# Narrow reciprocals and split float32r scores in the first attention of an encoder step

## The reference

```python
q = rope(q.reshape(b, t, N_HEADS_A, HEAD_DIM), pos)
k = rope(k.reshape(b, t, N_KV_A, HEAD_DIM), pos)
...
logit = jnp.einsum('bqgrd,bqkgd->bqgrk', qg, k_sel).astype(jnp.float32) * (HEAD_DIM ** -0.5)
logit = jnp.where(valid[:, :, None, None, :], logit, -jnp.inf)
p = jax.nn.softmax(logit, axis=-1).astype(v_sel.dtype)
o = jnp.einsum('bqgrk,bqkgd->bqgrd', p, v_sel)
```

## Time and profile before

| | |
|---|---|
| median of 3 runs | 1536.83 us (1536.07 to 1537.23) |
| the profiled execution's own time | 1536.02 us |
| its span in the trace | 1534.2 us |
| busy: PE / PE weight loads / DVE / ACT / GpSimd | 1491.9 / 1372.8 / 1081.5 / 635.9 / 580.2 us |
| chain that ended last, by engine | PE 86%, DVE 7%, ACT 2%, issue 2%, DMA 1% |
| granted TensorE clock, mean | 0.992 |
| first attention, from the first scores to the last products with values | 183.2 to about 290 us |

### The profile page before, as it was taken

How to read it: one execution, slowest core, us unless ns; L and a number is a source line. 1 busy time by engine, 2 the same in 40 slices (tenths; PEclk the granted TensorE clock), 3 DMA queues, 4 the chain that set the end, 5 groups by cost and what they waited for, 6 DMA issues and landing times.

```text
span 1534.2 us, 29121 instructions
## 1 busy us (share of the span) xinstructions
PE 1491.9 (97%) x11413; PEld 1372.8 (89%) x11413; DVE 1081.5 (70%) x2033; ACT 635.9 (41%) x1265; POOL 580.2 (38%) x346
## 2 busy tenths in 40 slices
PE   5999999999999999999999999999999999999998
PEld 2768955899999999999888888887999999999998
DVE  1559899768887878877634444457997877688753
ACT  3434366434552145532533333334254541355423
POOL 1234842134762066632222222231228640376421
PEclk8999999999999999999999999999999999999999
DMA  9874510232354433443254444442542355333521
GB/s 334 266 266 150 140 38 1 83 97 69 84 148 143 149 92 88 122 151 88 63 180 128 127 126 126 126 127 76 171 114 56 86 163 179 84 110 83 153 82 62
DMA packets 244455, 189.23 MB, mean 123 GB/s; under 512 B 12888, under 2 KB 228608, under 8 KB 240112
## 3 DMA queue, kind: packets, MB, share of 16 engines
q1 hardware_dynamic: 231232, 178.61, 38.8%
q10 hardware_dynamic: 13104, 8.97, 1.9%
HBM read 175.44 MB, written 8.50 MB: 120 GB/s over the span
## 4 chain that ended last, share of the span: by engine, by line
PE 86%; DVE 7%; ACT 2%; issue 2%; DMA 1%; POOL 0%; SPq 0%; POOLq 0%; ACTq 0%; DVEq 0%
PE lin L859 40%; PE lin L1438 28%; PE lin L876 6%; PE S L1200 2%; PE O L994 1%; PE O L1253 1%; DVE acc_out L2655 1%; PE O L1329 1%; PE T L1233 1%; DMA ada_raw<-in_w_ada 1%; PE S L1119 1%; PE S L1063 1%; DVE rinv_w L2555 1%; PE lin L1297 1%; PE S L1275 1%
## 5 line engine op out<-in xcount | busy, mean ns | idle before, releaser
L2145 POOL TENSOR_TENSOR w_lo<-w_raw,w_hi 128x1024 fp32r<-128x1024 f32 (+3 forms) x68 | 168.3, 2477 | 407.5 <-ACT w_hi L1610 407.5
L2236 POOL TENSOR_TENSOR w_lo<-ada_raw,w_hi 128x512 fp32r<-128x512 f32 x114 | 156.8, 1377 | 241.6 <-ACT w_hi L1911 241.6
L1610 ACT ACTIVATE w_hi<-w_raw 128x1024 fp32r<-128x1024 f32 (+2 forms) x110 | 125.1, 1139 | 225.0 <-PE lin L859 212.3
L859 PE MATMUL lin<-act_hi,w_hi 128*128 128x288 f32 (+1 forms) x1088 | 164.5, 302 | 6.1 <-ACT act_hi L1642 2.0
L859 PE MATMUL lin<-act_hi,w_lo 128*128 128x288 f32 (+1 forms) x1088 | 167.3, 299 | 0.2
L859 PEld LDWEIGHTS lin<-act_hi,w_hi 128*128 128x128 f32 (+1 forms) x1088 | 149.2, 189 | 16.6 <-issue 10.1
L859 PE MATMUL lin<-act_lo,w_hi 128*128 128x288 f32 (+1 forms) x1088 | 162.1, 298 | 0.0
L859 PEld LDWEIGHTS lin<-act_hi,w_lo 128*128 128x128 f32 (+1 forms) x1088 | 150.0, 188 | 7.5 <-issue 6.7
L859 PEld LDWEIGHTS lin<-act_lo,w_hi 128*128 128x128 f32 (+1 forms) x1088 | 149.6, 188 | 3.4 <-issue 2.9
L2236 POOL TENSOR_TENSOR w_lo<-s_tmp,w_hi 128x512 fp32r<-128x512 f32 x76 | 129.1, 1717 | 15.0 <-ACT w_hi L1914 14.9
L1438 PE MATMUL lin<-act_hi,w_hi 128*128 128x288 f32 x608 | 105.4, 295 | 0.0
(11 more groups left out here) (348 smaller groups left out, 3042.0 us busy)
## 6 DMA issues: line engine op xcount, KB each, us to landing
ada_raw<-in_w_ffn_in SPq DMA_DIRECT2D x76, 512.0 KB, 5.2
w_raw<-in_w_ffn_out SPq DMA_DIRECT2D x32, 704.0 KB, 4.8
ada_raw<-in_w_ada SPq DMA_DIRECT2D x20, 1024.0 KB, 7.8
ada_raw<-in_w_ada SPq DMA_DIRECT2D x32, 512.0 KB, 4.9
w_raw<-in_w_in_b SPq DMA_DIRECT2D x32, 512.0 KB, 4.2
w_raw<-in_w_in_a SPq DMA_DIRECT2D x16, 512.0 KB, 6.1
ada_qo<-in_w_ada SPq DMA_DIRECT2D x8, 1024.0 KB, 7.3
ada_raw<-in_w_ada_final SPq DMA_DIRECT2D x16, 512.0 KB, 5.6
```

Of the source, the lines that this page charges most:

```text
L859: last = nc.tensor.matmul(lin_u(u)[0:m, tok], w, (lo if p == 2 else hi)[:, at(t) if at else t, tok], start=(p == 0 and t == 0), stop=(p == ...
L1610: A(w_hi[:, u % 2, 0:n], w_raw[:, u % 2, 0:n], ACT.Copy).then_inc(whi_done, 1)
L2145: TT(w_lo[:, u % 2, 0:n], w_raw[:, u % 2, 0:n], w_hi[:, u % 2, 0:n].bitcast(F32), ALU.subtract)\
L2236: TT(ring(w_lo, q), raw, ring(w_hi, q).bitcast(F32), ALU.subtract).then_inc(ws_lo_p, 1)
```

## The change

1. Reciprocals. DVE makes them narrow (two or three columns, `recip_a`) and, after the softmax reads of unit n+2, copies them 64 times side by side (`widen_a`).
2. Scores. `kT4` becomes float32r and holds for each key head its high part on one half of the partitions and its low part on the other. A query head is needed on both halves: `q_hi` and `q_lo0`/`q_lo1` hold, for each of a pair's heads, the high and the low part on all 128 partitions. A score is then two float32r matmuls over 128 rows (high queries, low queries). The sample tokens of both heads lie side by side and make one product and one softmax read of 128 rows. `q_hi` and `q_lo0` share memory with `ada_raw`.
3. Who makes the parts. Keys: ACT the high parts (`k_high`, as many copies as before), GpSimd the low parts (`k_low`). Queries: pairs 0 to 2 by ACT (`q_high`) and DVE (`q_lows`: for pair 0 in the top-k rounds, for pairs 1 and 2 at the end of loop steps 0 and 2); pairs 3 to 7 by GpSimd (`q_split`, ahead of `split_pair` of the pair three before). The part on the other 64 partitions is brought by four DMAs a pair on the SP queue (`q_double`): pair 0's ahead of the load of U_Q+7, pair 1's ahead of the swap of U_Q+7, the others behind it.
4. The first `sum_load` waits for all scores (`s_done`) instead of `ada_used`.

```diff
+        q_hi = sb("q_hi", [P, 2, 2 * TOK], F32R, scope=s)
+        q_lo0 = sb("q_lo0", [P, 2 * TOK], F32R, scope=s)
...
-        kT4 = sb("kT4", [P, NG, NK], scope=a)
+        kT4 = sb("kT4", [P, NG, NK], F32R, scope=a)
...
+        Q_PARTS = [(0, 0, TOK, 0), (1, NP_, TOK, TOK), (1, 0, NP_, TOK + NS)]
...
-                    sp.wait_ge(ada_used, 3 * KT)
+                    sp.wait_ge(s_done, 4 * PAIRS)
...
+            def q_double(pair):
+
+                if pair < 3:
+                    sp.wait_ge(qhi_done, pair + 1)
+                sp.wait_ge(qlo_done, pair + 1)
+                for buf in (q_hi[:, pair % 2, :], q_low(pair)[:, :]):
+                    for e in range(2):
+                        own, other = slice(64 * e, 64 * e + 64), slice(64 - 64 * e, P - 64 * e)
+                        cols = slice(e * TOK, (e + 1) * TOK)
+                        sp.dma_start(buf[other, cols].bitcast(F32), buf[own, cols].bitcast(F32))\
+                          .then_inc(qdup_in[pair % 2], 16)
+
             for j in range(4, PAIRS):
                 q_load(j)
                 rope_swap(U_Q + j - 3)
+                if j == 6:
+                    q_double(0)
...
+            def last_queries(m):
+
+                if m < 3:
+                    rope_swap(U_Q + PAIRS - 3 + m)
+                if m == 1:
+                    q_double(1)
+                if m == 2:
+                    for pair in range(2, PAIRS):
+                        q_double(pair)
...
                 if n % 4 == 0:
-                    pe.wait_ge(rope_done, rope_of(U_Q + n // 4) + 1)
+                    pe.wait_ge(qdup_in[n // 4 % 2], 64 * (n // 8 + 1))
...
+                halves = (q_hi[:, pair % 2, :], q_low(pair)[:, :])
+                nk, col = (k + 1) * P, 384 if k == 0 else 0
+                for e in range(2):
+                    for j, q in enumerate(halves):
+                        last = nc.tensor.matmul(bank[:, e, col:col + nk], q[:, q_tile(e, k)],
+                                                kT4[:, pair // 2, 0:nk], start=(j == 0), stop=(j == 1))
                 if k == 0:
...
+                    for j, q in enumerate(halves):
+                        last = nc.tensor.matmul(bank[:, 0, 0:PAST + NS], q[:, NP_:NP_ + 2 * NS],
+                                                kT4[:, pair // 2, NP_:NK], start=(j == 0), stop=(j == 1))
                 last.then_inc(s_done, 1)
...
+            def q_high(pair):
+
+                act.wait_ge(rope_done, rope_of(U_Q + pair) + 1)
+                if pair == 0:
+                    act.wait_ge(ada_used, 3 * KT)
+                if pair >= 2:
+                    act.wait_ge(s_done, 4 * pair - 4)
+                for e, c0, c1, d0 in Q_PARTS:
+                    last = A(q_hi[64 * e:64 * e + 64, pair % 2, d0:d0 + c1 - c0], qo[64 * e:64 * e + 64, pair, c0:c1],
+                             ACT.Copy)
+                last.then_inc(qhi_done, 1)
...
+                if j in (3, 4):
+                    q_high(j - 3)
...
+                if n == 1:
+                    q_high(2)
...
+            def k_low(j):
+
+                for e in range(2):
+                    pool.wait_ge(khi_done, 4 * j + 2 * e + 1)
...
+                    for c0, c1, d0 in ((0, NP_, 0), (NP_, TOK, NP_ + PAST)):
+                        part = kT4[own, 2 * j + e, d0:d0 + c1 - c0]
+                        last = TT(part, kR[own, c0:c1], part.bitcast(F32), ALU.subtract)
+                    last.then_inc(klo_done, 1)
...
             split_lo(U_V + 1, N)
+            k_low(0)
             rope(U_K + 1)
...
                 split_lo(U_Q + j + 1, N)
+                if j == 2:
+                    k_low(1)
                 rope(U_Q + j - 2)
...
+            def q_split(pair):
+
+                pool.wait_ge(s_done, 4 * pair - 4)
+                for e in range(2):
...
+                    parts = [part for part in Q_PARTS if part[0] == e]
+                    for _, c0, c1, d0 in parts:
+                        last = CP(q_hi[own, pair % 2, d0:d0 + c1 - c0], qo[own, pair, c0:c1])
+                    last.then_inc(qhi_step, 1)
+                    pool.wait_ge(qhi_step, 2 * (pair - 3) + e + 1)
+                    for _, c0, c1, d0 in parts:
+                        last = TT(q_low(pair)[own, d0:d0 + c1 - c0], qo[own, pair, c0:c1],
+                                  q_hi[own, pair % 2, d0:d0 + c1 - c0].bitcast(F32), ALU.subtract)
+                    last.then_inc(qlo_done if e else qlo_half, 1)
...
             rope(U_Q + PAIRS - 1)
             for pair in range(PAIRS - 1):
+                if pair + 3 < PAIRS:
+                    q_split(pair + 3)
                 split_pair(pair)
...
+            def q_lows(pair):
+
+                dve.wait_ge(qhi_done, pair + 1)
+                for e, c0, c1, d0 in Q_PARTS:
+                    own = slice(64 * e, 64 * e + 64)
+                    last = V.tensor_tensor(q_low(pair)[own, d0:d0 + c1 - c0], qo[own, pair, c0:c1],
+                                           q_hi[own, pair % 2, d0:d0 + c1 - c0].bitcast(F32), ALU.subtract)
+                last.then_inc(qlo_done, 1)
+
             for it in range((TOPK_P - TOPK_S) // 8):
                 top_round(tiles[:3], 8 * (TOPK_S // 8), it)
+                if it == 2:
+                    q_lows(0)
...
-                if k == 0:
-                    V.reciprocal(rinv[:, 0, 2:3], rowsum[:, 0, 2:3])
-                V.reciprocal(rinv_w[:, k, :].rearrange("p (e c) -> p e c", e=2),
-                             rowsum[:, k, 0:2].rearrange("p (e a) -> p e a", a=1).broadcast_to([P, 2, HD]))\
+                w = 3 if k == 0 else 2
+                V.reciprocal(rinv[:, k, 0:w], rowsum[:, k, 0:w]).then_inc(recip_step, 1)
+
+            def widen_a(n):
+
+                k = n % 4
+                dve.wait_ge(recip_step, n + 1)
+                V.tensor_copy(rinv_w[:, k, :].rearrange("p (e c) -> p e c", e=2),
+                              rinv[:, k, 0:2].rearrange("p (e a) -> p e a", a=1).broadcast_to([P, 2, HD]))\
                     .then_inc(rinv_done, 1)
...
             for n in range(4 * PAIRS):
                 recip_a(n)
                 if n + 2 < 4 * PAIRS:
-                    max_unit((n + 2) % 4, n + 2, 0, 0, pr_a, ps_a, bias_a, bias_as, (S, S2)[n % 2])
+                    max_unit((n + 2) % 4, n + 2, 0, 0, pr_a, ps_a, bias_a, None, (S, S2)[n % 2])
+                widen_a(n)
                 if n % 4 == 0:
                     ta_evac(n)
                 if n >= 1:
                     out_a(n - 1)
                 if n % 4:
                     ta_evac(n)
+                if n in (0, 2):
+                    q_lows(1 + n // 2)
```

More of the change, by code:

```diff
@@ L507, in lin_u, with q_low, q_tile @@
             return lin[:, u % 2, :, :].rearrange("p b c -> p (b c)")[:, 512 - cut:512 - cut + TOK]
+        def q_low(pair):
+            return q_lo1 if pair % 2 else q_lo0
+        Q_PARTS = [(0, 0, TOK, 0), (1, NP_, TOK, TOK), (1, 0, NP_, TOK + NS)]
+        def q_tile(e, k):
+            c = k * P if e == 0 else TOK + NS + k * P
+            return slice(c, c + P)
         def rope_raw(u):
@@ L718, in out_stage_loads @@
                     w_load(u0 + m, w[:, m * P:(m + 1) * P], kt, P)
+                    if ahead is not None:
+                        ahead(m)
                     if m >= 1:
@@ L2496, in one @@
                                                   op0=ALU.add, op1=ALU.min, accum_out=acc)
-                if k == 0:
+                if k == 0 and bias_s is None:
+                    one(ps[:, :], bank[:, 0, 0:PAST + NS], sc[:, SOFF:], negmax[:, 0, 2:3])
+                elif k == 0:
                     for e in range(2):
```

74 lines of the change are left out of this document (42 added, 32 removed).

## The result

| | before | after |
|---|---|---|
| median of 6 runs each, us | 1536.82 (1536.07 to 1537.46) | 1543.53 (1542.12 to 1544.78) |
| ratio of the two, 95% interval | | 1.0044 (1.0034 to 1.0054) |
| profiled execution, us (span) | 1536.02 (1534.2) | 1544.48 (1542.7) |
| first scores of the second pair | 196.00 | 204.03 |
| first scores of the third pair | 207.56 | 218.12 |

The change makes the kernel slower, by 6.7 us. The page's sums say little of it: PE's busy time is nearly what it was (1491.9 before), and the chain has DVE at 10% where it had 7%.

What follows compares the result with a forecast made beforehand. The order of DVE's work was taken to hold PE back in the first attention's loop. Terms +1, +9, +3.5 and -4.5 made +9, with +1 for the clock +10: 1546.5 us from a profiled 1536.02, range 1533 to 1554.

Steps and rivals of the forecast that it cites:

- The case: The forecast itself, chance 0.49: slower, 1546.5 us, with PE stalled ahead of the second pair's scores.
- Front, +1: Ahead of the first attention: q_lows(0) holds GpSimd and q_double(0) delays the last query weights; +1 us (0 to 2.5).
- q_lows(1) and q_double(1), +9 beyond it: Second pair's scores wait for DVE subtractions in turns with GpSimd, SP issues and landing: +9 us (4.2 to 12).
- q_lows(2), +3.5: End of loop step 2: subtractions beside a rotation take 5.1 us, less 1.5 of DVE slack: +3.5 (0 to 5).
- the clock, +1: After the second pair's stall: PE likely at half clock for a few microseconds, +1 us, up to 4.
- Steady loop, -0.75 a pair: First attention's loop: earlier DVE work shortens three PE waits, -0.75 us a pair (0 to -1.3), in six undisturbed pairs.
- Taken: 0 more: Scores in the steady loop: float32r matmuls lose nothing, and the 0.6 us samples and k=0 save lie mostly beside a wait.
- DVE's relief: Steady loop: narrow reciprocals, cheap copies and one softmax read less free DVE of 2.7 us per pair.
- The rival in which GpSimd slows the loop: Pairs 3 to 7: widening copies wait for GpSimd, 7.5 us more, 1554; chance 0.09.
- The short stall, 0.25, at 1534: Rival, chance 0.25: subtractions slip between GpSimd's, start costs 4.2, q_lows(2) nothing, pairs return 5.3 to 7.7; most likely 1534.
- the 0.22 on faster: Chance given to a time below 1533.8 us, all of it from the short stall.
- After the attention, 0: Output stage: the w_ada loads, now behind the last scores, are wanted only there, priced 0.

Runs made afterwards that it cites:

- recip_alone: The kernel before with only the narrow reciprocals and widening copies; scores, keys and queries unchanged: 1535.28 us, ratio 0.9989.
- busy_in_stall: The changed kernel with 30 matmuls that nobody reads in the stall ahead of the second pair's scores: 1540.90 us, ratio 1.0028.
- high_first: The changed kernel with SP issuing the high-part doublings of pairs 0 to 2 before it waits for the low part: 1543.06 us, ratio 1.0039.
- gpsimd_waits_once: The changed kernel with GpSimd waiting for the second pair's low part before it rotates pair 5: 1541.14 us, ratio 1.0027.
- scores_alone: The changed kernel with the wide reciprocals put back: 1546.90 us, ratio 1.0064.
- gpsimd_waits_twice: The changed kernel with GpSimd waiting for the second pair's low part before rotating pair 5 and the third's before its last rotation: 1538.29 us, ratio 1.0011.
- low_by_gpsimd: The changed kernel with the low parts of the second and third pairs made by GpSimd: 1538.89 us, ratio 1.0015.
- recip_widen_late: recip_alone with unit 1's widening copy moved behind the scaling of the sample output: 1534.12 us, ratio 0.9987 to the kernel before.
- low_by_gpsimd_2: low_by_gpsimd with high_first's edit and GpSimd's part for pair 3 ahead of the last rotation: 1534.59 us, ratio 0.9987 to the kernel before.
- best: low_by_gpsimd_2 with recip_widen_late's edit: 1536.37 us, ratio 1.0001 to the kernel before.

## Why the prediction was right, and where its steps were off

**The case.** Slower with the stall where it was placed: PE waits for q_double(1), SP for the third subtraction, the subtractions for GpSimd. That mechanism was right and is tested above. The time came out 3.0 us below the forecast of 1546.5 (the median before and the sum's +10 give 1546.8), inside the range. That it came so near is in part luck: up to the end of the attention the sum is 3.9 us too high (10 for 6.1), and behind it 2.4 were lost in the profiled execution where it had nothing.

**Front, +1.** The first scores came 0.9 late and the third unit's 0.1 (191.78 for 191.69). Half of what was made good are the new scores of the two units between (0.4). recip_alone, which has nothing new ahead of the attention, has its first scores 0.5 late too, so a part of the 0.9 is no effect of the change. q_lows(0) took 5.40 for the forecast 5.1 and pushed DVE's first softmax read from 184.57 to 189.31. It was nearly hidden: PE waits 0.41 at 195.01 for an evacuation that DVE ends 0.7 later than before. The term was 0.1 at the third unit, so it was 0.9 too large.

**q_lows(1) and q_double(1), +9 beyond it.** 8.0 in all. The subtractions took 4.60 for 5.1 (turns of 3.0, not 3.5), the SP issues 2.4 and the landing 2.05, both as read from the earlier trace rows. They began at 194.88 for 195.

**q_lows(2), +3.5, and the clock, +1.** From the second pair's scores to the third's pass 14.09 us, 3.0 more than in a steady pair of the same kernel, where the two terms gave 4.5. PE's timeline shows both. From the first scores to those of k=1 it is 4.41 for 2.97, at half clock: 1.4, and 2.0 against busy_in_stall, so the clock's term was too small. Between the T and the sample transposes, which wait for DVE behind q_lows(2), it is 1.73 for 0.25: 1.5 in place of 3.5. That is the term most wrong in the sum. The step took 2.70 and not 5.1. GpSimd had been idle until 207.81, waiting for the swap behind q_double(1), and of its last rotation one operation ended at 209.2, just behind the start of q_lows(2) at 209.10: the first subtraction took 0.74 and paid no turn to speak of. The prediction had that swap queued there and took a full collision all the same. Where q_lows(2) began closer behind the start of the rotation the collision was fuller (3.74, 3.83, 3.94), PE's wait longer, and the clock fell again. So the third pair's scores came hardly earlier where the second's did: by 1.95 and -0.1 in high_first, by 3.6 and 0.8 in gpsimd_waits_once. The two delays hang together, and a sum that takes each by itself is too high.

**Steady loop, -0.75 a pair.** Measured -0.76 (11.87 to 11.11), and over the rest of the attention 10.56 - 6.1 = 4.5, the forecast's figure. The places are right as well: the transposes of k=2 come 0.28 earlier for the forecast 0.25, the T2 transposes of k=3 0.35 for 0.4, the rest gives 0.13 for 0.1. "Taken: 0 more" for the scores held, though for less than the prediction read: the sample and k=0 scores end 1.0 us behind their start where it had 0.6. The 0.39 of scores_alone is no contradiction. It is DVE's, by the one sample read less, which the sum counted under DVE. What was wrong is DVE's relief. In a steady pair of the changed kernel, DVE's timeline:

```profile
240.63 0.50 DVE L2674 COPY rinv_w<-rinv 128x128 f32<-128x128 f32 x1
...
242.91 0.71 DVE L2674 COPY rinv_w<-rinv 128x128 f32<-128x128 f32 x1
...
244.77 1.06 DVE L2674 COPY rinv_w<-rinv 128x128 f32<-128x128 f32 x1
...
247.97 0.22 DVE L2674 COPY rinv_w<-rinv 128x128 f32<-128x128 f32 x1
```

They take 0.22 with GpSimd idle and 0.50 to 1.06 beside it, 2.5 a pair for the forecast 1.08. DVE's relief is 11.10 - 9.52 = 1.6 and not 2.7. It was enough, since PE is idle in such a pair only once, ahead of the transposes of k=2, and there ACT's copy ends no earlier than DVE's:

```profile
241.60 0.52 PE L1334 MATMUL T<-consts,pr_a 128*128 128x128 f32 x3 [0.27 <-issue]
...
244.56 0.60 PE L1341 MATMUL lin<-consts,pr_a 128*128 128x128 f32 x4
```

The rival in which GpSimd slows the loop thus had its mechanism right, with a broadcast source as well, and its price wrong: the longer copies fall into DVE's own slack (it is idle 1.1 us ahead of the large scaling). In recip_alone, where the copy met GpSimd at another point, it did cost PE's time. That the changed kernel was spared this is luck as far as the prediction goes.

**The short stall, 0.25, at 1534.** gpsimd_waits_twice is that case made to order, and takes 1538.3. The second pair's scores come at 201.32, 5.3 late (5.0 counted from the third unit's scores), and 13.2 us pass to the third's, 1.6 more than before, where this rival gave 0. It left out the half clock behind a stall of 4.4 us (0.50 from 200 to 204) and q_lows(2)'s own 1.58. As priced, it would have crossed to faster at a loss of 5.3; with that very loss it is slower. Most of the 0.22 on faster stood on this mistake.

**After the attention, 0.** The profiled execution lost 6.1 us up to 296.4 and 8.5 in all. 1.5 of the rest are lost before ACT's first copy from `S` to `hid_hi`: it starts 109.4 us behind the attention's last scaling before, and 110.9 in the changed kernel. There the clock falls, to 0.83 and 0.50 in the two slices above. The kernel before has a smaller fall in the same place. Its windows:

```profile
340.00:345.00 5.00, 4.92 (x33) 4.55 (x32) 4.17 (x11) 2.26 (x5) 2.37 (x1) 0.80 0.35 105
345.00:350.00 5.00, 5.00 (x38) 5.00 (x37) 5.00 (x18) 4.03 (x13) 0.00 (x0) 0.86 0.86 236
```

There (1 - 0.80) x 5 + (1 - 0.86) x 5 = 1.7 us of full-speed work are missing, in the changed kernel 0.85 + 2.5 = 3.35. Not all of that is time: the stretch takes 109.3 to 109.8 us in four profiles with a fall of 1.7 (before, recip_alone, high_first, low_by_gpsimd) and 109.2 to 109.6 in three without any (recip_widen_late, low_by_gpsimd_2, best). So it is the larger fall that goes with the 1.5. The size of the fall differs from run to run, and no run shows whether the change makes it. The second attention, which the change does not touch, took 0.3 to 1.0 us longer in the profiles of recip_alone, recip_widen_late, low_by_gpsimd_2 and the changed kernel; why stays open.

## What to carry to other kernels

Count a DVE operation with two SBUF sources beside a busy GpSimd by instructions, here about 1 us of waiting each, and not by elements; and when it feeds a chain (subtraction, queue, landing) give it a place where its whole length, here 9 us, is covered. Before work is moved to another engine, lay out that engine's queue with due times: moving two low parts to GpSimd brought the second pair's scores 9 us earlier and lost 5 at the fourth pair to a rotation that nobody needed yet. Two parts of a change that are each worth little alone can be worth more together, and the other way round: look for the wait that each removes, and whether it is the same one. Two delays in a row are not to be added without asking whether the first one clears the way for the second.

## What the runs showed of the hardware that was not expected

- An SBUF copy whose source is broadcast (128x128 from 128x2) waits for GpSimd as well: 0.22 us alone, 1.07 beside it in recip_alone. By the Trainium skill (VectorE: DVE Perf Modes, Mode 2×_2P) a copy can use both read ports. The trace fits that, by the wait of 0.85 us; which ports this copy uses no row shows.
- PE's granted clock was 0.50 (1.2 GHz) behind waits of 4.4 us (gpsimd_waits_twice: 0.50 in the window from 200 to 204) and of 7.46 us; with matmuls that nobody reads in the wait it stayed at 1.00. It fell behind shorter waits too, of 2.34 us (high_first, 0.57 from 212 to 216) and 2.54 us (busy_in_stall, 0.53).
- Eleven executions of one kernel can differ by 6.0 us (busy_in_stall, 1538.55 to 1544.50), while eleven of recip_alone lie within 1.3. Whether the second fall of the clock makes the difference is not shown.
